# A hybrid decoder block on one Trainium2 core: gates by feature, scans for running sums, and the memory turned by VectorE

## The reference

```python
h = rmsnorm(x, norm_mix_w)
proj = h @ w_in                    # hq, hf, hi, hgate, gq, gk, gv, ggate, glr
f = lb + (1 - lb) * sigmoid(hf)    # lb: one number per feature, 512 of them
hk, hlogf = 1 - f, log(f)          # keys and log decay of HGRN2 (4 heads of 128)
o_hg = chunked_gated_recurrence(silu(hq), hk, hi, hlogf, 1.0)
gdecay = log_sigmoid(glr @ gla_w_gk2 + gla_b_gk) / 16      # GLA, 4 heads of 64
o_gla = chunked_gated_recurrence(gq, gk, gv, gdecay, 64 ** -0.5)
# inside the recurrence: b = cumsum(g) over the tokens of each chunk of 64
...
x = x + cross_attend(rmsnorm(x, norm_xa_w), rmsnorm(mem, norm_mem_w), w_xq, w_xkv, w_xo)
x = x + moe(rmsnorm(x, norm_moe_w), ...)   # top 4 of 32 experts
```

## Time and profile before

| | |
|---|---|
| median of 3 runs | 1188.64 us (1188.61 to 1191.11) |
| the profiled execution | 1188.46 us, its span 1186.7 us |
| TensorE busy | 1137.7 us, 96% |
| VectorE busy | 379.4 us, 32% |
| ScalarE busy | 175.2 us, 15% |
| GpSimd busy | 19.0 us, 2% |
| HBM read | 443.20 MB, 374 GB/s over the span |
| mean granted TensorE clock | 0.987 |

### The profile page before, as it was taken

How to read it: one execution, slowest core, us unless ns; L and a number is a source line. 1 busy time by engine, 2 the same in 40 slices (tenths; PEclk the granted TensorE clock), 3 DMA queues, 4 the chain that set the end, 5 groups by cost and what they waited for, 6 DMA issues and landing times.

```text
span 1186.7 us, 18637 instructions
## 1 busy us (share of the span) xinstructions
PE 1137.7 (96%) x7483; PEld 572.1 (48%) x7484; DVE 379.4 (32%) x896; ACT 175.2 (15%) x366; POOL 19.0 (2%) x58
## 2 busy tenths in 40 slices
PE   9999999999999999999999999999999999999997
PEld 5988879855443443334333333333333333333332
DVE  4688878545222111122212121111111111111112
ACT  5311421243100000001000000000000000000002
POOL 3000010000000000000000000000000000000000
PEclk9999999999999999999999999999999999999999
DMA  9954203989999999999999999999999999999995
GB/s 306 380 196 144 73 10 120 350 334 383 420 426 434 430 429 432 426 436 429 435 430 430 435 428 436 430 434 430 433 432 429 436 428 436 429 434 423 426 424 222
DMA packets 42853, 444.89 MB, mean 375 GB/s; under 512 B 6308, under 2 KB 6772, under 8 KB 26040
## 3 DMA queue, kind: packets, MB, share of 16 engines
q1 hardware_dynamic: 41912, 441.63, 88.9%
q0 software_dynamic: 480, 1.85, 0.7%
q10 hardware_dynamic: 416, 0.79, 0.2%
HBM read 443.20 MB, written 1.05 MB: 374 GB/s over the span
## 4 chain that ended last, share of the span: by engine, by line
PE 68%; DMA 30%; DVE 1%; ACT 0%; SPq 0%; issue 0%; DVEq 0%; ACTq 0%
DMA ring<-in_w_gate_up 30%; PE bank L1168 23%; PE bank L1159 13%; PE bank L733 7%; PE bank L729 4%; PE bank L1198 4%; PE bank L1213 3%; PE bank L712 2%; PE bank L873 1%; PE bank L1095 1%; PE bank L1284 1%; PE bank L1189 1%; PE bank L1275 1%; PE bank L1007 1%; PE bank L1129 1%; PE bank L1087 1%
## 5 line engine op out<-in xcount | busy, mean ns | idle before, releaser
L1168 PE MATMUL bank<-ring,region 128*64 128x512 f32 x2048 | 464.2, 608 | 36.4 <-DMA ring<-in_w_gate_up 36.4
L1168 PEld LDWEIGHTS bank<-ring,region 128*64 128x64 f32 x2048 | 147.1, 140 | 333.9 <-issue 268.6
L1159 PE MATMUL bank<-ring,region 128*64 128x512 f32 x1024 | 226.8, 596 | 0.3 <-ACT region L1407 0.3
L2290 DVE TENSOR_SCALAR region<-bank 128x512 f32<-128x512 f32 x32 | 22.1, 692 | 570.4 <-PE bank L1168 570.4
L1159 PEld LDWEIGHTS bank<-ring,region 128*64 128x64 f32 x1024 | 71.2, 137 | 130.0 <-issue 127.2
L1407 ACT ACTIVATE region<-bank 128x256 f32<-128x256 f32 (+1 forms) x134 | 55.4, 440 | 369.0 <-PE bank L1159 251.0
L733 PE MATMUL bank<-ring 128*128 128x256 f32 x392 | 86.6, 381 | 0.0
L1407 ACT ACTIVATE bank<-region 128x512 f32<-128x512 f32 x32 | 19.2, 601 | 453.1 <-DVE region L2290 453.1
L733 PEld LDWEIGHTS bank<-ring 128*128 128x128 f32 x392 | 73.9, 190 | 10.9 <-issue 0.7
L1198 PE MATMUL bank<-region 64*128 64x512 f32 x264 | 65.6, 615 | 0.1
L1213 PEld LDWEIGHTS bank<-region,r_levels 128*128 128x128 bf16 x1536 | 61.2, 117 | 1.6 <-issue 1.6
(11 more groups left out here) (300 smaller groups left out, 761.4 us busy)
## 6 DMA issues: line engine op xcount, KB each, us to landing
ring<-in_w_gate_up SPq DMA_DIRECT2D x48, 4096.0 KB, 30.2
ring<-in_w_down SPq DMA_DIRECT2D x24, 4096.0 KB, 37.0
ring<-in_w_gate_up SPq DMA_DIRECT2D x26, 2048.0 KB, 15.2
ring<-in_w_down SPq DMA_DIRECT2D x10, 2048.0 KB, 14.3
ring<-in_w_in SPq DMA_DIRECT2D x6, 2048.0 KB, 17.3
ring<-in_w_gate_up SPq DMA_DIRECT2D x11, 1024.0 KB, 35.7
ring<-in_w_xkv SPq DMA_DIRECT2D x4, 2048.0 KB, 10.9
ring<-in_w_down SPq DMA_DIRECT2D x7, 1024.0 KB, 9.1
```

The costliest lines, as they stand in the source:

```text
L1159: last = pe.matmul(bk[half * ROWS:(half + 1) * ROWS, :], lhs, w[:, half * 512:(half + 1) * 512], start=start, stop=stop, skip_group_check= ...
L1168: last = pe.matmul(rows, lhs, columns[:, half], start=start, stop=stop, skip_group_check=True)
L2290: v.tensor_scalar(g_t, bank_g[:, :], LIMIT, None, ALU.min).then_inc(sem["g_clamped"], 1)
```

## The change

The forget products, `z` and the gates come out by feature, so nothing is transposed back; the running sums are `tensor_tensor_scan` on VectorE, with a mask that starts anew at each chunk; `glr` and `z` work on rows that are already scaled. The memory is loaded with a quarter of its features on each 32 partitions (runs of 1 KB), squared by ScalarE in eight pieces, its sums over the four partition groups come from one small product (`mem_sum`), GpSimd scales and weighs it, and VectorE turns it in two instructions of 32x32 blocks. The bounds `lb` and the gate's bias are loaded as columns, in 4-byte pieces. The new order of jobs and the core of the diff:

```diff
-JOBS = (["xT00", "xT01", "hf0", "xT10", "xT11", "hf1", "glr", "rms_row"] + four("mT") + ["z", "hq0", "hq1", "fT0", "fT1", "b0", "b1", "b2"] + five("gs")
+JOBS = (["xT00", "xT01", "hf0", "hf1", "xT10", "xT11", "rms_row", "mem_sum", "hq0", "glr", "z", "hq1"] + five("gs")
...
             sp.dma_start(w_glr, A["w_in"][0, :, C_GLR:C_GLR + RANK].rearrange("(p k) n -> p k n", k=KT)).then_inc(sem["glr_in"], 16)
-            sp.dma_start(mem_raw, A["mem"][0].rearrange("(t p) n -> p t n", p=P)).then_inc(sem["mem_in"], 16)
-            sp.dma_start(w_mem, by_row(A["norm_mem_w"][0])).then_inc(sem["w_mem_in"], 16)
+            sp.dma_start(lb_raw, A["hg_lb_logits"].rearrange("a (m p) -> p a m", p=P)).then_inc(sem["cols_in"], 16)
+            for q in range(4):
+                sp.dma_start(mem_rows[q * PAD:(q + 1) * PAD], A["mem"][0].rearrange("(b i) n -> i b n", i=PAD)[:, :, q * QUARTER:(q + 1) * QUARTER]).then_inc(sem["mem_in"], 16)
+            sp.dma_start(w_mem, by_row(A["norm_mem_w"][0])).then_inc(sem["cols_in"], 16)
+            sp.dma_start(gk_bias[:, 0:2], A["gla_b_gk"][0].rearrange("(m p) -> p m", p=P)).then_inc(sem["cols_in"], 16)
             sp.wait_ge(sem["pads_zeroed"], 1)
             for row in range(0, P, PAD):
                 sp.dma_start(gk2[row:row + RANK, :], A["gla_w_gk2"][0]).then_inc(sem["glr_in"], 16)
-            sp.dma_start(lb2, A["hg_lb_logits"].rearrange("(o a) n -> o a n", o=1).broadcast_to([P, 2, 512])).then_inc(sem["lb_in"], 16)
-            sp.dma_start(gk_bias, A["gla_b_gk"].broadcast_to([P, 256])).then_inc(sem["gk_bias_in"], 16)
...
-            sem_last = pool.memset(tri[0:1, CHUNK:CHUNK + 1], 0.0)
-            sem_last.then_inc(sem["consts_ready"], 1)
+            link(pool.memset(same_row, 0.0))
+            for first in range(0, P, PAD):
+                link(pool.affine_select(out=same_row, in_=same_row, compare_op=ALU.not_equal, fill=1.0, base=-first,
+                                        pattern=[[0, P // PAD], [-1, PAD]], channel_multiplier=1))
+            link(pool.memset(keep_mask, 1.0))
+            link(pool.memset(keep_mask[:, ::CHUNK], 0.0))
+            pool.memset(tri[0:1, CHUNK:CHUNK + 1], 0.0).then_inc(sem["consts_ready"], 1)
...
-            for job in ("b0", "b1", "b2"):
-                wait_full(pool, job)
+            pool.wait_ge(sem["mem_rms"], 1)
+            for b in range(0, 8, 4):
+                rows = mem_rows[:, b:b + 4, :]
+                pool.tensor_tensor(rows, rows, mem_rstd[:, b:b + 4].unsqueeze(2).broadcast_to([P, 4, QUARTER]), ALU.mult).then_inc(sem["mem_scaled"], 1)
+            pool.wait_ge(sem["mem_turned"], 2)
+            pool.wait_ge(sem["cols_in"], 48)
+            for k in range(0, KT, 4):
+                rows = memT[:, k:k + 4, :]
+                pool.tensor_tensor(rows, rows, w_mem[:, k:k + 4].unsqueeze(2).broadcast_to([P, 4, T]), ALU.mult).then_inc(sem["mem_weighed"], 1)
+            pool.wait_ge(sem["scanned"], 1)
             pool.memset(s_t[:, :], 0.0).then_inc(sem["s_zeroed"], 1)
...
-            w, rows_bank = panel(0), [begin("hf0")]
-            for k0, k1 in zip(FIRST_ROWS, FIRST_ROWS[1:]):
-                pe.wait_ge(first_in[FIRST_ROWS.index(k0)], 16)
+            w, forget_bank = panel(0), [begin("hf0"), begin("hf1")]
+            def forget(k0, k1, first, last, m):
+                bk = forget_bank[m // 2]
+                for k in range(k0, k1):
+                    await_rows({0: [f"xT{first // P}0"], 4: [f"xT{first // P}1"]}, k)
+                    ins = pe.matmul(bk[:, m % 2 * T + first:m % 2 * T + last], w[:, k, m * P:(m + 1) * P], hT[:, k, first:last],
+                                    start=(k == first == m % 2 == 0), stop=(k == KT - 1), skip_group_check=True)
+                return ins
+            for i, (k0, k1) in enumerate(zip(FIRST_ROWS[:2], FIRST_ROWS[1:3])):
+                pe.wait_ge(first_in[i], 16)
                 for t in range(NT):
                     if (t, k0) == (1, 0):
                         flip_x(1)
-                        rows_bank.append(begin("hf1"))
+                    for m in range(4):
+                        ins = forget(k0, k1, t * P, (t + 1) * P, m)
+            ins.then_inc(sem["hf_streamed"], 1)
+            pe.wait_ge(sem["consts_ready"], 1)
+            pe.wait_ge(sem["x_diag"], NT)
+            bk = begin("rms_row")
+            for t in range(NT):
+                last = pe.matmul(bk[:, t * P:(t + 1) * P], ones[:, :], x_diag[:, t, :], start=True, stop=True)
+            end(last, "rms_row")
+            pe.wait_ge(first_in[2], 16)
+            for job in ("xT01", "xT11"):
+                wait_taken(pe, job)
+            for m in range(4):
+                ins = forget(*FIRST_ROWS[2:], 0, T, m)
+                if m % 2 == 1:
+                    end(ins, f"hf{m // 2}")
+            pe.wait_ge(sem["mem_squared"], 1)
+            end(pe.matmul(begin("mem_sum")[:, 0:8], same_row, mem_sums, start=True, stop=True), "mem_sum")
+            w = arrived("w_in", C_HQ)
+            query_bank = begin("hq0")
+            def queries(k0, k1):
+                for i in range(2):
                     for k in range(k0, k1):
-                        await_rows({0: [f"xT{t}0"], 4: [f"xT{t}1"]}, k)
...
+                        last = pe.matmul(query_bank[:, i * T:(i + 1) * T], w[:, k, i * P:(i + 1) * P], hT[:, k, :],
+                                         start=(k == i == 0), stop=(k == KT - 1), skip_group_check=True)
+                return last
+            pe.wait_ge(sem["hT_scaled"], 1)
+            queries(0, KT // 2)
+            pe.wait_ge(sem["hT_scaled"], 2)
             pe.wait_ge(sem["glr_ready"], 1)
             bk = begin("glr")
             groups = P // PAD
...
                     k = groups * j + g
                     last = pe.matmul(bk[g * PAD:(g + 1) * PAD, 0:T], glr_padded[:, k, :], hT[:, k, :], start=(j == 0),
                                      stop=(j == KT // groups - 1))
-            end(last)
...
+            end(last, "glr")
+            end(queries(KT // 2, KT), "hq0")
             wait_taken(pe, "glr")
             bk = begin("z")
-            for t in range(NT):
...
+            for m in range(2):
+                last = pe.matmul(bk[:, m * T:(m + 1) * T], gk2[:, m * P:(m + 1) * P], glrT, start=True, stop=True)
+            end(last, "z")
             by_feature("hq1", w, 2, hT)
-            pe.wait_ge(sem["f_ready"], NT)
...
             w = arrived("w_in", C_GQ)
...
-            for job in four("mT"):
-                wait_taken(pe, job)
+            pe.wait_ge(sem["mem_weighed"], 2)
...
-            act.wait_ge(sem["mem_in"], 16)
...
             nc.scalar.preload_act_table_set("sigmoid_and_others")
-            remember(0)
-            remember(1)
-            take("glr", glrT, bank_of("glr")[:, 0:T])
             take("rms_row", rms_row, bank_of("rms_row")[:, 0:T])
             act.wait_ge(sem["lb_diff"], 1)
-            fn(lb2[:, 0, :], lb2[:, 0, :], ACT.Sigmoid).then_inc(sem["lb_sigmoid"], 1)
+            fn(lb, lb_raw[:, 0, :], ACT.Sigmoid).then_inc(sem["lb_sigmoid"], 1)
+            act.wait_ge(sem["mem_in"], 16 * 4)
+            for b in range(8):
+                ins = fn(r_t[:, b * QUARTER:(b + 1) * QUARTER], mem_rows[:, b, :], ACT.Square, scale=ROOT, accum_out=mem_sums[:, b:b + 1])
+            ins.then_inc(sem["mem_squared"], 1)
+            for i in range(2):
+                wait_taken(act, f"hf{i}")
+                fn(sigT[:, 2 * i:2 * i + 2, :], sigT[:, 2 * i:2 * i + 2, :], ACT.Sigmoid).then_inc(sem["first_sigmoids"], 1)
+            act.wait_ge(sem["lb_diff"], 2)
+            act.wait_ge(sem["first_sigmoids"], 2)
+            for m in range(HEADS):
+                ins = fn(gT[:, m, :], sigT[:, m, :], ACT.Ln, scale=lb_rest[:, m:m + 1], bias=lb[:, m:m + 1])
+            ins.then_inc(sem["lnf_ready"], 1)
+            take("glr", glrT, bank_of("glr")[:, 0:T])
+            def query_sigmoid(i):
+                wait_full(act, f"hq{i}")
+                fn(tmp[:, i, :], bank_of(f"hq{i}")[:, :], ACT.Sigmoid).then_inc(sem["first_sigmoids"], 1)
+            query_sigmoid(0)
             act.wait_ge(sem["z_abs"], 1)
             fn(ez, ez, ACT.Exp).then_inc(sem["z_ln"], 1)
             act.wait_ge(sem["z_ln"], 1)
             fn(l_z, ez, ACT.Ln, bias=1.0).then_inc(sem["z_ln"], 1)
...
+            query_sigmoid(1)
...
-            for t in range(NT):
...
+            dve.wait_ge(sem["cols_in"], 48)
+            v.tensor_tensor(lb_raw[:, 0, :], lb_raw[:, 0, :], lb_raw[:, 1, :], ALU.subtract).then_inc(sem["lb_diff"], 1)
+            def scale_rows(h):
                 rows = hT[:, 4 * h:4 * h + 4, :]
                 v.tensor_tensor(rows, rows, rms_row.unsqueeze(1).broadcast_to([P, 4, T]), ALU.mult).then_inc(sem["hT_scaled"], 1)
-            dve.wait_ge(sem["gk_bias_in"], 16)
...
+            def scale_forget(i):
+                wait_full(dve, f"hf{i}")
```

(54 more changed lines are left out.)

139 lines of the change are left out of this document (26 added, 113 removed).

## The result

| | before | after |
|---|---|---|
| median of 15 runs each (lowest to highest), us | 1188.64 (1187.67 to 1191.24) | 1192.74 (1191.26 to 1193.66) |
| profiled execution, us / its span, us | 1188.46 / 1186.7 | 1193.62 / 1191.9 |
| start of gs / of hi on the chain, us | 43.77 / 56.27 | 41.53 / 61.80 |

A forecast was written before the change was run, and what follows sets the result against it. TensorE bounds the kernel until 571.50 us, then a stream of expert weights whose start depends on TensorE's signals. TensorE's net 5.1 us less 0.6 for hand-overs gave 1188.5 - 4.5 = 1184.0 us; range 1183.0 to 1192.0.

The forecast's parts named there:

- rival A: GpSimd and VectorE operations exclude each other, so TensorE waits 6.4 to 8.3 us in gs; 1191.4 us, chance 0.31.
- B: Rival: VectorE late by its own scans and transposes at double price; TensorE waits 2.3 us in gs; 1186.3, chance 0.18.
- Net 5.1 us: TensorE's start: three removed groups save 5.31 us, mem_sum adds 0.2; gs starts at 38.7 instead of 43.77.
- Panel lands at 21.9, wanted at 23.0: Load of hq's weight panel: about 0.5 us earlier than the 22.4 before, so TensorE need not wait.
- C: Rival: hq's panel or mem_sum late, short runs at three times their price; 1.3 us wait at 23 us; 1185.3, chance 0.05.
- Scans and transposes at the lower end: VectorE before gs: priced like two-input operations of their size, 1.22, 0.69 and twice 1.22 us; doubled, 4.35 us more.
- VectorE waits for none of it: GpSimd's four memory operations, 2.1 us each, off the chain, finish at 31.7, before VectorE's transposes from 34.1.
- the slack of 2.0: VectorE before gs's combine_weights: 0.9 us up to the sigmoid and 1.1 behind it, for all unknown operations.
- the 0.6 that the forecast held for hand-overs: Deduction from TensorE's 5.1 us gain for hand-overs that no profile row prices, leaving 4.5 us.

The follow-up runs named there:

- f_early: c_best with the Newton steps for the memory's 1/rms moved to where VectorE waits for ScalarE's logarithm of the gates; 1185.77 us, ratio 0.9985.
- g_split: f_best with ScalarE's memory scaling in pairs around its keeping of gs products, first transpose behind the second level's differences; 1184.00 us, ratio 0.9961.
- a_queues: The changed kernel with half of the memory's loads issued from ScalarE's queue instead of SyncE's; 1193.37 us, ratio 1.0038 to the kernel before.
- a_scale: The changed kernel with ScalarE instead of GpSimd scaling and weighing the memory; 1186.81 us, ratio 0.9992 to the kernel before.
- b_read: The kernel before plus two GpSimd multiplications of 1024 columns on a scratch tile, beside VectorE's scaling of the activations; 1188.63 us, single run.
- c_order: a_scale with the queries' panel issued before the memory, and the memory's sum, Newton steps, scaling and transposes behind the queries; 1191.40 us, ratio 1.0018.
- c_best: c_order with the logits loaded by ScalarE's queue and ScalarE setting the memory's features apart for contiguous transposes; 1191.42 us, ratio 1.0017.
- a_both: The changed kernel with the edits of a_scale and a_queues together; 1187.48 us, ratio 0.9985 to the kernel before.
- f_hold: c_order with GpSimd's clearing of the score buffer also waiting for the end of the memory's Newton steps; 1186.78 us, ratio 0.9986.
- d_rows: a_scale with each of the four memory loads going to all 128 partitions instead of 32, shuffling the memory's rows; 1187.01 us, single run.
- e_turn: a_scale with VectorE's two block transposes reading consecutive elements instead of every eighth, so features change order; 1185.24 us, single run.
- f_best: f_early with the second queries behind gs's combined weights, and the transposes and the memory's weighing later; 1185.55 us, ratio 0.9982.

## Why the prediction was wrong

The forecast was 1184.0 with 0.43, the kernel after took 1192.74: rival A, priced at 1191.4 and held possible with 0.31, is what happened. B's longer operations and a slower clock, which neither the forecast nor a rival had priced, came on top of it, and it ended 0.7 us above the range. Step by step:

- **"Net 5.1 us", TensorE.** Right. The three groups are gone from the chain, and in f_early, where neither the panel nor VectorE delays it, gs starts at 38.8, as laid out. g_split, which keeps these edits of TensorE and of the scans, reached the forecast number, but with GpSimd's work moved, the panel moved and hi at 52.4 instead of 51.2 (38.7 + 12.5); that it is the same to the tenth is luck.
- **"Panel lands at 21.9, wanted at 23.0".** Wrong: 25.34. I priced packets and took the panel's issue to stay at 11.01; it went to 15.79, behind eleven issues where there had been eight, of which the first two took 4.25 and 3.18 us. That loads into 32 partitions run at 181 to 222 GB/s, not at the panels' 383, was not in the reckoning at all. The first query product started at 25.39, 2.4 us later than predicted, and with 0.4 of small gaps behind it gs at 41.53 instead of 38.7. C had 0.05. In this kernel it cost nothing, though (a_queues), because VectorE was later still.
- **"Scans and transposes at the lower end".** Mis-sized: 2.28 and 1.22 us instead of 1.22 and 0.69, transposes 1.97 each instead of 1.22; 3.1 us more, of the 4.35 that B allowed. The Trainium skill ("DVE: opcode table, instruction layouts, handler registers and perf-mode slots", Datapath and trigger behaviour) has the scan at half throughput; the trace agrees with it (2.28 against 1.22 us).
- **"VectorE waits for none of it", GpSimd.** The step that failed: the forecast put four GpSimd operations beside VectorE and charged VectorE nothing for them. GpSimd's own price was right for the first pair (3.89/2 = 1.95 us, predicted 2.1; the second took 5.01/2). But each pair lengthened two VectorE operations, 6.35 us in all (A said 8.4), and without them the wait in gs is gone (a_scale).
- **The sum of these.** 6.35 + 3.1 less the slack of 2.0, less the 2.8 by which gs itself was later, gives 4.6 us of wait; 4.95 were measured. (VectorE also began this stretch at 23.4 instead of 22.8, which the sum leaves out.)
- **The clock.** No term of mine had it: in the kernel after, the clock is at 1.2 GHz when the wait of 4.95 us ends and stays there until about 55.5, which costs another 2.8 us. So a wait of TensorE there costs more than its length. In all 2.8 (gs later) + 4.95 + 2.8 = 10.6 us at the start of hi; less the 0.6 that the forecast held for hand-overs and the 0.3 by which the span grew less than hi moved (5.2 against 5.5 us), that is 9.7, and the profiled run ended 9.6 above 1184.0.

Why A had only 0.31: the evidence was one pair of selects (0.67 and 0.29 us), and the forecast set against it that GpSimd might slip in between PSUM operations. It could not, since the operations at stake work in SBUF, where b_read shows them held up.

## What to carry to other kernels

An idle engine is no free helper if its operations and those of the engine that bounds the stretch hold each other up: look at which VectorE operations will run beside each GpSimd operation, those with one SBUF input and plain memsets included, and let one of the two wait on purpose. When a load is split or added ahead of a weight panel, count issues in the queue, not bytes alone: here putting the panel first was worth the whole wait. And price a wait of TensorE with the slower clock that may follow it: it followed all waits of 3.94 to 4.95 us here (after, a_queues, c_order, c_best), and some of the shorter ones (1.46 in a_both, 2.25 in f_hold, 2.41 in d_rows), but not others (1.54 in e_turn, 1.78 in f_best, 2.06 in a_scale, 2.31 in a_queues).
